# A two-block model on one core: ScalarE swaps the halves of the S5 additions and states, VectorE turns whole rows; transfers on SyncE; early pair scores

## What is computed

```python
u, z = split(h @ w_in)                         # S5: 2048 channels each
bu = complex(einsum(u, real(b_bar)), einsum(u, imag(b_bar)))   # 128 groups of 16 channels, 64 states
states = scan(x[t] = lam_bar * x[t-1] + bu[t])                 # complex, along 512 tokens
y = einsum(real(states), c_re) - einsum(imag(states), c_im) + d * u
y = gelu(y); y = y * sigmoid(y @ w_glu + b_glu) * silu(z)

k_mla = concat(k_nope, broadcast(rope(k_r), 8 heads))          # attention of the second block
p = softmax(q @ k.T + mask or selection); o = p @ v
```

## Time and profile before

| | |
|---|---|
| median of three runs | 1732.74 us (1732.45 to 1734.89) |
| the profiled execution | 1733.98 us, its span 1732.1 us |
| mean granted clock of TensorE | 0.985 |
| busy: TensorE, VectorE, ScalarE, GpSimd | 1671.1, 1003.2, 675.1, 584.9 us |
| chain of work that ended last | TensorE 80%, VectorE 11%, ScalarE 4% |
| S5 batches | 443 to about 800 us |
| start of the pairs of the attention | 1191.93 us |

### The profile page before, as it was taken

The page is one execution under the profiler, slowest core; times in us unless marked ns, Lnnn a source line. Parts: engine busy times, 40 slices in busy tenths (PEclk is TensorE's granted clock), DMA queues, the critical chain, the costliest instruction groups (busy, mean ns, idle before and its releaser), DMA issues.

```text
span 1732.1 us, 22888 instructions
## 1 busy us (share of the span) xinstructions
PE 1671.1 (96%) x9208; PEld 1336.3 (77%) x9208; DVE 1003.2 (58%) x1526; ACT 675.1 (39%) x964; POOL 584.9 (34%) x205
## 2 busy tenths in 40 slices
PE   7999999999999997999999999998999999999997
PEld 5777788888788886777888887686677888887876
DVE  4356535786988889984563645797963222222123
ACT  4473323333443446444333323326673322222222
POOL 2231013443543332000344331233774333443432
PEclk8999999999999998999999999998999999999999
DMA  5223003335754565645744321112002333332322
GB/s 170 74 97 97 1 25 98 97 97 152 144 131 127 128 140 110 115 101 165 255 140 133 97 71 50 49 43 86 2 1 73 98 97 89 86 94 82 94 84 82
DMA packets 266670, 167.85 MB, mean 97 GB/s; under 512 B 88923, under 2 KB 246838, under 8 KB 266438
## 3 DMA queue, kind: packets, MB, share of 16 engines
q1 hardware_dynamic: 239504, 142.27, 30.6%
q10 hardware_dynamic: 26614, 22.25, 4.8%
q0 software_dynamic: 448, 1.88, 0.3%
HBM read 144.86 MB, written 16.78 MB: 93 GB/s over the span
## 4 chain that ended last, share of the span: by engine, by line
PE 80%; DVE 11%; ACT 4%; issue 2%; ACTq 1%; DMA 1%; SPq 1%; POOL 0%; DVEq 0%; POOLq 0%
PE PS L702 23%; PE PS L703 22%; PE PS L704 22%; DVE ring_lo L1999 2%; PE PA L920 1%; ACTq L1650 1%; PE PA L917 1%; PE PS L1284 1%; PE PA L894 1%; PE PS L1296 1%; PE PA L1268 1%; PE PA L1130 1%; DMA ring<-in_gla_w_in 1%; DVE PB L2607 1%; PE PA L1143 1%
## 5 line engine op out<-in xcount | busy, mean ns | idle before, releaser
L2687 POOL TENSOR_TENSOR ring_lo<-ring,ring_hi 128x2048 fp32r<-128x2048 f32 (+2 forms) x91 | 398.0, 4374 | 942.2 <-ACT ring_hi L1411 942.1
L1411 ACT ACTIVATE ring_hi<-ring 128x2048 fp32r<-128x2048 f32 (+3 forms) x122 | 222.2, 1827 | 200.5 <-PE PS L704 172.1
L703 PE MATMUL PS<-U3l,ring_hi 128*128 128x512 f32 x352 | 140.0, 398 | 0.0
L702 PE MATMUL PS<-U3h,ring_hi 128*128 128x512 f32 x352 | 139.5, 396 | 0.0
L704 PE MATMUL PS<-U3h,ring_lo 128*128 128x512 f32 x352 | 139.0, 395 | 0.0
L2644 DVE TENSOR_TENSOR SF<-PS,rs 128x512 f32<-128x512 f32 x22 | 15.2, 691 | 162.8 <-PE PS L704 162.7
L702 PE MATMUL PS<-HT5h,ring_hi 128*128 128x512 f32 x256 | 106.4, 416 | 3.0 <-DVE ring_lo L1999 2.9
L1999 DVE TENSOR_TENSOR ring_lo<-ring,ring_hi 128x2048 fp32r<-128x2048 f32 x31 | 93.8, 3040 | 20.1 <-ACT ring_hi L1411 19.9
L704 PE MATMUL PS<-HT5h,ring_lo 128*128 128x512 f32 x256 | 101.5, 396 | 0.0
L703 PE MATMUL PS<-HT5l,ring_hi 128*128 128x512 f32 x256 | 101.3, 396 | 0.0
L1909 ACT ACTIVATE SF<-SF 128x512 f32<-128x512 f32 x22 | 13.9, 632 | 174.2 <-DVE SF L2644 174.2
(11 more groups left out here) (490 smaller groups left out, 4218.6 us busy)
## 6 DMA issues: line engine op xcount, KB each, us to landing
ring<-in_gla_w_in SPq DMA_DIRECT2D x20, 1024.0 KB, 5.2
ring<-in_s_w_in SPq DMA_DIRECT2D x16, 1024.0 KB, 5.8
ring<-in_s_w_glu SPq DMA_DIRECT2D x16, 1024.0 KB, 6.1
ring<-in_w_gate SPq DMA_DIRECT2D x22, 512.0 KB, 4.0
ring<-in_w_up SPq DMA_DIRECT2D x22, 512.0 KB, 5.3
ring<-in_w_down SPq DMA_DIRECT2D x16, 704.0 KB, 4.4
ring<-in_w_in SPq DMA_DIRECT2D x9, 1024.0 KB, 5.2
ring<-in_gla_w_out SPq DMA_DIRECT2D x8, 1024.0 KB, 5.8
```

The lines of the kernel that those rows point to most:

```text
L702: pe.matmul(dst, w[0], x[0], start=start, stop=False)
L703: pe.matmul(dst, w[0], x[1], start=False, stop=False)
L1411: act.activation(ring_hi[:, n % NSLOT, 0:plan.size[n]], ring[:, n % NSLOT, 0:plan.size[n]], ACT.Copy)\
L2687: pool.tensor_tensor(ring_lo[:, n % NSLOT, at], ring[:, n % NSLOT, at], ring_hi[:, n % NSLOT, at].bitcast(F32), ALU.subtract).then_inc(wlo ...
```

## The change

- **S5, swap.** ScalarE copies the additions crosswise from PSUM (`swap_additions`, two copies of 64x512) and, after the scan, the states (`swap_states`, two of 64x520) into `swapped`, half of `sq`. VectorE turns all 128 rows at once. While ScalarE copies the states, VectorE does scaled of the first tile and add_skip.
- **S5, order on VectorE.** b_factors(b+2) moves from ahead of the scan to behind scaled of the second tile; only in batches 0 to 7 the first of LOWS[b] stays ahead of that.
- **S5, transfers.** KM's eight transfers move from ScalarE to SyncE, except for batch 0.
- **S5, last batch.** The first glu_a tile of S5_LAST is computed around by_feature(15).
- **Attention.** The scores of pairs 0 and 1 are issued between the ukvv tiles, the exponentials of pair 0 between their copies; the rotary part of Km is copied by ScalarE in four parts instead of VectorE (L2583); the high part of attn_out's weights moves on ScalarE to pair 24, the low part on GpSimd behind the pairs; single rounds of `select` go with pairs 3 to 26 instead of 1 to 24; the last pair's multiplication is VectorE's, and its transposes go to PA.

```diff
+            def swap_additions(b):
+                act.wait_ge(v_ps, b + 1)
+                if b > 0:
+                    act.wait_ge(m_ready, b)
+                for to, of in (HALF_ROWS, HALF_ROWS[::-1]):
+                    ins = act.activation(swapped[to, 0:T], PA[of, 3, :], ACT.Copy)
+                ins.then_inc(v_swapped, 1)
+
+            def swap_states(b):
+                act.wait_ge(summed_states, SWAPS + b + 1)
+                for to, of in (HALF_ROWS, HALF_ROWS[::-1]):
+                    ins = act.activation(swapped[to], M_tmp[of].rearrange("p g n -> p (g n)"), ACT.Copy)
+                ins.then_inc(m_swapped, 1)
...
+                swap_additions(b)
                 if b + 1 < NBATCH:
                     b_rows(b + 1, 0)
                 split_weights(s5_used[b] + 2)
...
                 if b + 2 < NBATCH:
                     columns(b + 2)
+                swap_states(b)
...
-                for to, of in (half_rows, half_rows[::-1]):
-                    ins = tt(turned[to], v[of], rot_s[of, :, 0:NB], ALU.mult)
+                link(tt(turned, swapped[:, 0:T].rearrange("p (g n) -> p g n", g=BG), rot_s[:, :, 0:NB], ALU.mult))
...
-                for to, of in (half_rows, half_rows[::-1]):
-                    link(tt(M[to], M_tmp[of], rot_s[of], ALU.mult))
-                link(tt(M_tmp[:], M_tmp[:], rot_c[:], ALU.mult))
-                tt(M[:], M[:], M_tmp[:], ALU.add).then_inc(m_ready, 1)
+                link(tt(M[:], M_tmp[:], rot_c[:], ALU.mult))
+                beside()
+                dve.wait_ge(m_swapped, SWAPS + b + 1)
+                link(tt(M_tmp[:], swapped.rearrange("p (g n) -> p g n", g=BG), rot_s[:], ALU.mult))
+                tt(M[:], M[:], M_tmp[:], ALU.subtract).then_inc(m_ready, 1)
...
-                if b + 2 < NBATCH:
-                    b_factors(b + 2)
...
-                for n in LOWS[b]:
+                for n in LOWS[b][:1] if b < GA else ():
                     low_weights(n)
                 for tile in own_tiles[1:2]:
                     scaled(*tile)
+                if b + 2 < NBATCH:
+                    b_factors(b + 2)
                 if b + 2 in DVE_STATES:
                     state_factors(b + 2)
+                for n in LOWS[b][1 if b < GA else 0:]:
+                    low_weights(n)
...
+            def inner_rows(b):
+                sp.wait_ge(gs_ready, b + 1)
...
             def beside_batch(b):
+                if b >= 1:
+                    inner_rows(b)
                 if 1 <= b and b + 1 < NBATCH:
                     u_loads(b + 1)
```

```diff
+                if i < EARLY:
+                    scored(i)
...
+            for i, tile in enumerate(tiles["ukvv"]):
+                if i == 1:
+                    exponentials(0)
...
+                if p == OUT_SPLIT:
+                    split_weights(tiles["attn_out"][0].loads[0])
...
-            split_weights(tiles["attn_out"][0].loads[0])
-            for n in range(2 * MH * NPAIR):
+            split_weights(tiles["ukvv"][0].loads[0])
+
+            for n in range(2 * MH * NPAIR - 2):
```

More of the change, by code:

```diff
@@ L1068, in pe_program @@
                     inside(b + 1)
+                else:
+                    dense(*S5_LAST[0], 0, 4)
                 dense(*beside[1], k, KD)
@@ L1073, in pe_program @@
                     dense(*beside[2], 0, KD)
-            for stage, m in S5_LAST:
+            dense(*S5_LAST[0], 4, KD)
+            for stage, m in S5_LAST[1:]:
                 dense(stage, m, 0, KD)
@@ L1231, in pe_program @@
                     rotate(FIRST_QR + i)
[L1232 to L1243, removed]
             def scored(p):
@@ L1271, in scored @@
                 m.then_inc(score_ps, 1)
+            EARLY = 2
+            w = parts_view(tiles["ukn"][0].loads[0], (MH * P,))
+            pe.wait_ge(pad_zero, 4)
+            for i, tile in enumerate(tiles["ukn"]):
+                feature_tile(tile, lambda k: both(w, slice(None), slice(i * P, (i + 1) * P)),
+                             lambda k: (CKh[:, 0:T2], CKl[:, 0:T2]), 1, T2)
+            for i, tile in enumerate(tiles["ukvv"]):
+                open_tile(tile)
+                for b in range(2 if i < 2 else 1):
+                    t0 = (2 * i + b) * P
+                    m = product(PS[:, 2 * tile.slot + b, :], (CKh[:, t0:t0 + P], CKl[:, t0:t0 + P]),
+                                both(w, slice(None), slice(MH * MNOPE, MH * P)), True, True)
+                m.then_inc(tile_done, 1)
+                if i < EARLY:
+                    scored(i)
             def transposed(p):
                 i = PAIRS[p][1]
[L1275 to L1278, removed]
+                if p == 0:
+                    for tile in tiles["ukvv"][-2:]:
+                        read_out(pe, tile)
+                to = turned_banks(p)
+                if to is PS:
+                    if p > 0:
+                        pe.wait_ge(pT_sb, p)
+                    if i + 2 > 4 and p >= 2:
+                        pe.wait_ge(oa_ready, p - 1)
                 for h in range(2):
@@ L1298, in with_values @@
                 ins.then_inc(pv_out_ps, 1)
-            for p in range(len(PAIRS) + 3):
+            for p in range(EARLY, len(PAIRS) + 3):
                 if p < len(PAIRS):
@@ L1863, in exponentials @@
                                    accum_out=mx[:, n % 6, 1:2]).then_inc(exp_ready, 1)
+            for i, tile in enumerate(tiles["ukvv"]):
+                if i == 1:
+                    exponentials(0)
+                act.wait_ge(tile_done, tile.t + 1)
+                nb = 2 if i < 2 else 1
+                act.activation(Vm[:, 2 * i:2 * i + nb, :], PS[:, 2 * tile.slot:2 * tile.slot + nb, :], ACT.Copy).then_inc(slot_free[tile.slot], 1)
             def copy_transposed(p):
                 i = PAIRS[p][1]
+                of = turned_banks(p)
                 act.wait_ge(pT_ps, p + 1)
@@ L2319, in scan @@
                 dve.wait_ge(rot_used, b + 1)
-                link(tt(own, own, turned, ALU.subtract))
+                link(tt(own, own, turned, ALU.add))
                 dve.wait_ge(dk_ready, b + 1)
-                link(dve.tensor_tensor_scan(M_tmp[:].rearrange("p g n -> p (g n)"), M[:].rearrange("p g n -> p (g n)"),
-                                            dk[:].rearrange("p g n -> p (g n)"), 0.0, ALU.add, ALU.mult))
-                for to, of in (half_rows, half_rows[::-1]):
-                    link(tt(M[to], M_tmp[of], rot_s[of], ALU.mult))
@@ L2617, in dve_program @@
             assert chosen[0] == NPAIR * (TOPK // 8)
-            for i in range(4):
+            output(len(PAIRS) - 4)
+            for n in (2 * len(PAIRS) - 2, 2 * len(PAIRS) - 1):
+                dve.wait_ge(p_ready, n)
+                dve.wait_ge(rsum_ready, n + 1)
+                nk = keys(PAIRS[n // 2][1])
+                ts(PB[:, n % 6, 0:nk], PB[:, n % 6, 0:nk], mx[:, n % 6, 2:3], None, ALU.mult).then_inc(p_ready, 1)
+            for i in range(1, 4):
+                low("oa", i - 1, OA[:, i - 1, :], OAh[:, i - 1, :], OAl[:, i - 1, :])
                 output(len(PAIRS) - 4 + i)
-                low("oa", i, OA[:, i, :], OAh[:, i, :], OAl[:, i, :])
+            low("oa", 3, OA[:, 3, :], OAh[:, 3, :], OAl[:, 3, :])
             def ffn_low(i):
```

79 lines of the change are left out of this document (44 added, 35 removed).

## The result

| | before | changed |
|---|---|---|
| median | 1732.6 us (4 runs) | 1772.7 us (4 runs) |
| range of the runs | 1729.56 to 1734.89 | 1770.88 to 1773.80 |
| ratio to before, 95% interval | | 1.0232 (1.0213 to 1.0250) |
| span of the profiled execution | 1732.1 | 1771.5 |
| mean granted clock | 0.985 | 0.974 |

The account below looks back on a forecast made before the run. TensorE, busy 96% of the span, was taken as the bound, so only its idle stretches and granted clock count. Terms 29 + 9 - 7 + 3 - 7.3 = +26.7 on 1733.98 gave 1760.7, median 1759.5 us, range 1727 to 1772.

Parts of the forecast that it names:

- VectorE against GpSimd, batches 0 to 7: S5 scan: GpSimd's state factors hold VectorE's last product and subtraction, 2.6 us later per batch; +29 us with ScalarE's lags.
- C: The time in an S5 batch when ScalarE's CZ ends; with GpSimd in the way the subtraction ends at C + 5.3.
- Batch 8 and the start of 9: S5: ring_lo behind b_factors makes TensorE wait 5.5 us, +5, and batch 8 is itself late by 3.9: together +9.
- Batches 10 to 15: Late S5, forecast as batches 9 to 15: KM's transfers leave ScalarE, WB copies come in time, VectorE's chain is shorter: -7.
- Clock in S5: Granted clock behind the new waits of 2.6 to 5 us: most harmless, +3, bounds 0 and 11, 1.4 to 1.7 a fall.
- Attention: Start of the attention: first transposes 5.1 us earlier, 2.6 of low clock back, copy wait -0.4, rotary copies +0.8: -7.3.
- The lags without GpSimd: S5: ScalarE's late copies overrun TensorE's cover by 0, 0.7, 0.7 and 1.4, some 2 in batch 0: 8 us in all.
- the batch sums: S5 output waits: 2.6 (batches 3, 7), 3.3 (1, 4, 5), 3.9 (2, 6), about 5 (0), plus 0.6 in 2, 4, 6.
- the likeliest case: Whole kernel: the forecast itself, GpSimd holding VectorE's short products, 1759.5 us, alone spanning 1748 to 1772; chance 0.50.
- the case without exclusion: S5 rival: GpSimd doesn't meet VectorE's short products, 8 instead of 29 and 6.4 instead of 9; 1733, no change; chance 0.22.
- the faster one: S5 rival: CZ comes early enough that the copies stay inside TensorE's 10.2 us of other products; -9.5, 1723; chance 0.18.
- worse: S5 rival: nearly each new wait lowers the clock, 8 more at 1.4, and GpSimd's third product holds too; 1770; chance 0.10.

Follow-up runs that it names:

- run 6: Changed kernel with GpSimd's state factors of batch b + 2 behind VectorE's b_factors(b + 2), and batch 8's first ring_lo ahead: 1738.0 us, ratio 1.0017.
- run 9: Changed kernel with ScalarE's crosswise copies of the states moved ahead of the ring_hi parts and tile_out: 1728.9 us, ratio 0.9971 to before.
- run 1: Changed kernel with GpSimd starting the state factors of batch b + 2 only when the states of batch b are ready: 1763.3 us, ratio 1.0153.
- Run 8: Kernel before with only KM's transfers moved to SyncE: 1728.4 us, ratio 0.9959.
- run 5: Changed kernel with 9 to 22 overwritten matmuls filling most of each wait ahead of the outputs of batches 0 to 8: 1764.2 us, ratio 1.0161.
- Run 2: Changed kernel with the first ring_lo of batch 8 also moved ahead of scaled of the second tile and b_factors: 1764.3 us, ratio 1.0159.
- run 3: Kernel before with only the attention part of the change: 1729.8 us, ratio 0.9970.

## Why the prediction was wrong

The direction and the mechanism were right, the size wasn't: 1759.5 forecast, 1772.7 measured, 0.7 us above the range. By its terms:

- **VectorE against GpSimd, batches 0 to 7: +29 forecast, waits +24.1 measured.** The states came at C + 5.2 for a forecast C + 5.3. The output waits are 27.0, 1.7 of which were there before; small waits for ring_lo, 2.3, went and 1.2 for WB came. Runs 6 and 9 bear the exclusion out: with GpSimd elsewhere the two instructions take 0.70. By the Trainium skill ("SBUF — State Buffer", section "SBUF: two separate sides") whichever of the two engines starts first holds the shared port pair for its whole instruction, and these rows agree. Subtracting run 1 doesn't split ScalarE's part from GpSimd's, because GpSimd's time goes to whichever instruction is next. The rows of run 6 do: ScalarE's order is 4.1 us in batches 1 to 7, forecast 4.9.
- **Batch 8 and the start of 9: +9 forecast, waits +9.3** up to additions(10), (12.3 against 3.1), the outputs of batch 9 among them.
- **Batches 10 to 15: -7 forecast, -7.7** from additions(10) to additions(15). Run 8 gives 2.5 of it to the transfers alone; the rest needs the new scan and order.
- **Clock in S5: "I take most as harmless: +3, bounds 0 and 11". This step failed.** It cost 14.2 us up to additions(8), shown by run 5, and by the same subtraction 6.5 more up to additions(10) (15.8 longer, waits 9.3), **20.7** in all. Run 2, which removes one wait there, gives back 4.1 beyond the waits in that stretch; the rest of the 6.5 is by subtraction alone. I had taken "dense products directly behind" a wait as protection. They aren't directly behind it: the outputs' small matmuls and inside(b+1) come first, 4.0 us in batch 4 (580.54 to 584.58), as they did behind the 2.2 us wait that had lowered the clock in the kernel before. Behind eight of the first nine output waits it fell, and since TensorE is the bound in these batches, each fall was on the path.
- **Attention: -7.3 forecast, -5.5** by run 3 (interval -2.6 to -7.8). In the changed kernel the stretch from the first value tile to the end is 538.0 us instead of 544.9, -6.9. The clock still falls behind its first transposes, 0.76 from 1240 to 1245.
- The profiled execution also lost 2.2 us ahead of the S5 batches, where nothing was changed, and took 2.3 less between additions(15) and the first value tile.

From additions(0) to additions(15): 24.1 + 9.3 - 7.7 + 20.7 = 46.4, measured 384.9 - 338.6 = 46.3. The clock term alone was 18 us too low; that the total was only 13 off is partly luck, since the early waits came out 5 us shorter than forecast.

Three of the prediction's own workings don't hold. The lags without GpSimd, as listed, add up to 6.9 and not 8, and the batch sums to 29.7, of which 1.7 was there before. Clock 11 instead of 3 would take the likeliest case to 1767.5 and not to 1772, so the range ended where its terms didn't reach. And the swap isn't what exposes the last turn to GpSimd: its half-row product had both operands in SBUF before too (L2325); what is new is that it comes behind CZ, as GpSimd does. Run 9, which keeps the operands and moves the copies ahead of CZ, shows this. For the additions' product the operand did move, and run 6 shows it held.

The rivals: the short products were held, so the case without exclusion fell, and batches 2 and 6 are late by 1.2 to 1.3 us in run 6 although nothing of their scan is held, so the faster one fell too; "worse" named the right cause, with 1.4 us a fall where 2.0 were measured, and gave 1770.

## What to carry to other kernels

On a TensorE-bound kernel a wait costs more than its length: where a change puts a wait of 2.5 us or more into each turn of a loop, count the low clock behind every one of them (here about 2 us each, 14.2 for seven falls in eight batches), unless rows show it stay up behind such waits in the same place. A helper's copies belong in its engine's list where the waiting engine wants them, not behind the steps that happened to be there: one call moved was worth 44 us here (run 9), low clock included. And look which instructions of GpSimd start at the same event as the new VectorE work; delaying them moves the collision (run 1), and helps as far as it then falls where VectorE is idle (run 6).

## What the runs showed of the hardware that I had not expected

- VectorE's tensor_scalar of 128x520, one operand in SBUF, is held too: 2.14 us beside GpSimd's product in run 1 instead of 0.43. So not only products of two SBUF operands are.
- The length of a wait doesn't settle the clock: behind 3.16 us in batch 5 the granted clock was 1.00 to 621 us, behind 2.52 and 2.51 in batches 3 and 7 it was 0.58 and 0.59 in the next 3 us. Why batch 5 was spared no run shows.
